# Banded lag products for a causal convolution and causal pooling, with token tiles arranged by phase

## The chip, the cores and the metric

The kernel runs on one core of a Trainium2 chip. The metric is the device time of one execution in microseconds. Each version is timed over several runs, and one execution is profiled.

## What is computed

One layer of a hybrid encoder on x of 2048 tokens by 1024 channels, in float32:

```
x  = LayerNorm(x)
h  = x @ w_in                       # 1024 -> 384 value | 384 gate | 384 pool | 256 query
a  = h_value * sigmoid(h_gate)
a  = causal_depthwise_conv(a, 31 taps) + bias
a  = silu(LayerNorm over the 384 channels of a)
p  = (trailing mean over 2/4/8/16 tokens, by group of 96 channels) - h_pool
p  = (p @ pool_w of its group) * scale
mo = 4-head attention from h_query into 256 memory tokens
y  = concat(a, p, mo) @ w_out
x  = LayerNorm(alpha * x + y)
u  = causal_depthwise_conv(x @ w_up, 3 taps) + bias   # 1024 -> 2 x 2816
y  = (silu(u_gate) * u_value) @ w_down
x  = LayerNorm(alpha * x + y)
```

The means of the first tokens divide by the number of tokens seen so far, not by the window.

## The kernel before

Every large product is made from three TensorE products. Each operand is split into a high part (a copy in the engine's 32-bit format, ScalarE) and a low part (the subtraction of the high part, VectorE), and high x high, high x low and low x high are summed in PSUM (`exact_parts`, L37). Each phase is a block of programs, one per engine, tied by semaphores. SP issues all DMAs. Order on an engine is program order.

**Input phase** (`input_phase`, L73). Four chunks of 512 tokens. At the start four tiles of x are normalised (statistics and affine on VectorE, L412 to L428; the reciprocal root on POOL; the scaling on ScalarE, L319), turned by TensorE (`turn`, L256) and split (L324, L441), and w_in is loaded in eight rows of 1408 columns, split at L371 and L528. TensorE then runs `project` (L281): 11 column tiles of 24 matmuls each. ScalarE evacuates them (`evacuate`, L326). The conv has three tiles of 128 channels. Two are convolved on VectorE, 31 steps of `scalar_tensor_tensor` per tile and chunk (`conv`, L458, the step at L473). The third is convolved on TensorE: ScalarE scales the identity by a tap's high and low part (`tap_matrix`, L346), and TensorE does 3 matmuls of 512 columns per tap (`last_tile_conv`, L269, matmul at L278), between the turns of the next chunk. Pooling runs on VectorE by doubling the window (`pool_level`, L484). Results go to the scratch `mix_d`, channels by tokens. The next chunk's LayerNorm stands ahead of the conv on VectorE.

**Mixing phase** (`mixing_phase`, L562). First the preparation: memory, key, value, pool and output weights are loaded (L730 to L753) and split (`prep_low` L1226, `wout_hi` L1044, `wout_lo` L1230). TensorE makes the keys (L918), folds the pool weights into the output weights (L935) and makes the values (L944). Then eight chunks of 256 tokens: scores, softmax, attention, the LayerNorm and swish of the conv result, the output projection, the residual and its LayerNorm. `chunk` (L949, L1083, L1269) gives the hand-written order of each engine: the projection of one chunk is mixed with the attention of the next. Chunk 0 runs without a projection beside it, and TensorE waits for all eight output weight tiles ahead of chunk 1 (`pe.wait_ge(wo_l, KT)`, in the lines after L949). x1 and sums of its quarters are stored.

**FFN phase** (`ffn_phase`, L1332). Both large products by a scheme of seven half-size products instead of eight (`product`, L1664). The up projection is done in two stages of 1024 tokens with 22 blocks each; a block is one 128-channel tile of gate and of value. Its width-3 conv is one ScalarE step (`first_tap`, L1764) and two VectorE steps for each of the two windows (`conv`, L1883), reading the tile shifted by 0, 1 and 2 columns. Two columns are saved to and restored from `up_carry` between the stages (`save_edge` L1752, `restore_edge` L1758). `keep_u2` (L1727) copies the second product, and TensorE waits for it ahead of the fourth.

The order of TensorE around a chunk of the input phase:

```
with pe.Fori(0, NCH - 1) as c:
    project(c)
    for n in range(2 * TT):
        turn(c + 1, n)
        for k in range(4 * n, min(4 * n + 4, CONV_K)):
            last_tile_conv(c, k)
project(NCH - 1)
for k in range(CONV_K):
    last_tile_conv(NCH - 1, k)
```

Of the kernel before, what the change touches and what calls it, by code (L numbers as in the profile page):

```python
# [5 lines left out]
F32 = mybir.dt.float32  # L6
# [56 lines left out]
POOL_ROWS = []  # L63
for _g, _w in enumerate(POOL_WINDOWS):
    _c = _g * POOL_GROUP
    while _c < (_g + 1) * POOL_GROUP:
        _p = _c % P
        _n = min((_g + 1) * POOL_GROUP - _c, P - _p, {0: 128, 32: 32, 64: 64, 96: 32}[_p])
        POOL_ROWS.append((_c // P, _p, _n, _w))
        _c += _n  # L70


def input_phase(nc, a, x0_d, mix_d, used):  # L73

# [4 lines left out]
    HALO = CONV_K - 1  # L81
    PH = max(POOL_WINDOWS)
    DT = CT - 1
    RING = 4
    GATE_AT, LOW_AT = 9, 12
    with ExitStack() as ctx:
        sb = lambda n, s, d=F32: ctx.enter_context(nc.sbuf_tensor(n, s, d))
        
# [5 lines left out]
        xt_hi = sb("x0t_hi", [P, KT, CH], F32R)  # L94
        xt_lo = sb("x0t_lo", [P, KT, CH], F32R)
        xs = sb("x_in", [P, 2, D])
        x0 = sb("x0", [P, TT, D])

        glu = sb("glu", [P, DT, HALO + CH])
        glt_hi = sb("glu_last_hi", [P, HALO + CH], F32R)  # L100
        glt_lo = sb("glu_last_lo", [P, HALO + CH], F32R)

        diag = sb("tap_diag", [P, RING, 2, P], F32R)
        cwt_hi = sb("tap_hi", [P, CONV_K], F32R)
        cwt_lo = sb("tap_lo", [P, CONV_K])

        vg = sb("val_gate", [P, 2, CT, PH + CH])

        cp = sb("conv_pool", [P, 2, CT * CH])
        pin = sb("pool_in", [P, CT, PH + CH])  # L110
        qb = sb("q_out", [P, QT, CH])
        g_b = sb("ln0_gb", [P, 2, D])
        cw = sb("conv_w", [P, CT, CONV_K])
        cb = sb("conv_b", [P, CT])
        ident = sb("ident0", [P, P])
        half = sb("rstd_consts0", [P, 2])
        st = sb("ln0_stats", [P, TT, 16])
        rc = sb("pool_recip", [P, CT, PH])
        rw = sb("pool_recip_full", [P, CT, PH])
        ptmp = sb("pool_head", [P, CT, PH])  # L120
# [3 lines left out]
        x_loaded = [sem(f"x_loaded{i}") for i in range(2)]  # L124
        x_first = [sem(f"x_first{i}") for i in range(TT)]
        raw_loaded = [sem(f"win_loaded{i}") for i in range(5)]
        consts = sem("consts0")
# [4 lines left out]
        ln_stats = sem("ln0_stats_done")  # L132
        ln_var = sem("ln0_var")
        half_ok = sem("half0_ok")
        pchain = sem("pool_chain0")
        x0_norm = sem("x0_norm_done")
        x0_ready = sem("x0_ready")
        x0_stored = [sem(f"x0_stored{i}") for i in range(TT)]
# [5 lines left out]
        conv_done = sem("conv_done")  # L144
        taps_hi = sem("taps_hi_done")
        taps_lo = sem("taps_lo_done")
        diag_ready = sem("diag_ready")
        last_gated = sem("glu_last_done")
        glt_hi_done = sem("glu_last_hi_done")
        glt_lo_done = sem("glu_last_lo_done")  # L150
        halo_hi = sem("halo_hi_done")
        tap_mm = sem("tap_mm_done")
        last_conv = sem("last_conv_done")
        pool_done = sem("pool_done")
        conv_stored = sem("conv_stored")
        pool_stored = sem("pool_stored")
        last_stored = sem("last_conv_stored")
        q_stored = sem("q_stored")
        chain = sem("dve_chain0")
        block = ctx.enter_context(nc.Block())  # L160


        order = [v for t in range(CT) for v in (t, CT + t)] + list(range(2 * CT, JT))

        def load_x(sp, c, u):
            if isinstance(c, int) and c == 0:

                sp.dma_start(x0[:, u, :], a["x"][u * P:(u + 1) * P, :]).then_inc(x_first[u], 16)
                return

            if not (isinstance(c, int) and c == 1 and u < 2):
                sp.wait_ge(x0_norm, c * TT + u - 1)
            sp.dma_start(xs[:, u % 2, :], a["x"][bass.ds(c * CH + u * P, P), :]).then_inc(x_loaded[u % 2], 16)

        def store_x0(sp, c, u):
            sp.wait_ge(x0_ready, c * TT + u + 1)
            sp.dma_start(x0_d[bass.ds(c * CH + u * P, P), :], x0[:, u, :]).then_inc(x0_stored[u], 16)

        def store_mix(sp, c):

            at = c * CH if isinstance(c, int) else sp.snap(c * CH)

            def rows(r, n):
                return mix_d[r:r + n * P, bass.ds(at, CH)].rearrange("(t p) s -> p t s", p=P)
            sp.wait_ge(conv_done, DT * (c + 1))
            sp.dma_start(rows(0, DT), cp[:, 0, 0:DT * CH].rearrange("p (t s) -> p t s", t=DT)).then_inc(conv_stored, 16)
            sp.wait_ge(evac, JT * (c + 1))
            sp.dma_start(rows(D_CONV + D_POOL, QT), qb[:, :, :]).then_inc(q_stored, 16)
            sp.wait_ge(pool_done, c + 1)
            sp.dma_start(rows(D_CONV, CT), cp[:, 1, :].rearrange("p (t s) -> p t s", t=CT)).then_inc(pool_stored, 16)  # L190
            sp.wait_ge(last_conv, c + 1)
            sp.dma_start(mix_d[DT * P:D_CONV, bass.ds(at, CH)], cp[:, 0, DT * CH:]).then_inc(last_stored, 16)

# [5 lines left out]
        def _(sp):  # L199
            def load_w(k):  # L200
                if k >= len(landing):

                    sp.wait_ge(win_lo, k - len(landing) + 1)
# [1898 lines left out]
```

## Time and profile before

| | |
|---|---|
| median of 3 runs | 2083.57 us (2080.91 to 2083.67) |
| profiled execution | 2081.61 us, its span 2079.8 us |
| TensorE busy | 1915.2 us, 92% of the span, 8584 matmuls |
| VectorE busy | 1637.7 us, 79% |
| ScalarE busy | 984.5 us, 47% |
| POOL busy | 218.6 us, 11% |
| mean granted TensorE clock | 0.969 |
| DMA | 282.96 MB, mean 136 GB/s |

The span is the time from the first to the last instruction. Busy times overlap, because the engines run side by side; a matmul's busy time includes its way through the pipeline, so the pitch from start to start says more. A granted clock of 1.00 is 2.4 GHz, 0.50 is 1.2 GHz. "Idle before" is the idle time of the engine ahead of the instructions of a row, with what ended it.

### The profile page before, as it was taken

To read this page: it belongs to the slowest core of one execution; us is meant where nothing else is said; L and a number is where in the kernel's file an instruction comes from. 1 tells how busy PE (TensorE), PEld (TensorE's weight loads), DVE (VectorE), ACT (ScalarE), POOL (GpSimd) and SP (SyncE) were. 2 spreads that over 40 slices of the span, in tenths; PEclk is the share of its full clock that TensorE was granted. 3 is DMA by queue.
4 is the path that set the end of the run, shared out by engine and by line. 5 is a ranking of instruction groups with operands and counts; after the bars stand their busy time and mean duration, and the time that the engine had idled before them with its cause. 6 is when DMAs were issued, how large, how long until landed. Compare 5 with 4: busy or idle time off the path is not lost.

```text
span 2079.8 us, 26573 instructions
## 1 busy us (share of the span) xinstructions
PE 1915.2 (92%) x8584; PEld 1580.4 (76%) x8584; DVE 1637.7 (79%) x2241; ACT 984.5 (47%) x1681; POOL 218.6 (11%) x263
## 2 busy tenths in 40 slices
PE   3999999669999849999999999999999798999997
PEld 2887878558878638888888778888888686887786
DVE  7979877568898557888888788777778767656899
ACT  4264351555555345555555655555555434324231
POOL 1010100001122201222122001000000000000111
PEclk9999999789999969999999999999999899999999
DMA  6130210523443363334434524222214557547543
GB/s 247 67 114 27 81 41 1 195 91 110 144 151 116 131 239 112 134 139 141 141 123 149 202 102 142 83 89 91 81 71 142 186 203 267 190 170 263 183 162 121
DMA packets 135506, 282.96 MB, mean 136 GB/s; under 512 B 10512, under 2 KB 66960, under 8 KB 135440
## 3 DMA queue, kind: packets, MB, share of 16 engines
q1 hardware_dynamic: 135440, 282.13, 38.3%
q8 instruction: 35, 0.57, 0.1%
q14 instruction: 31, 0.25, 0.0%
HBM read 182.48 MB, written 99.61 MB: 136 GB/s over the span
## 4 chain that ended last, share of the span: by engine, by line
PE 54%; DMA 4%; DVE 3%; issue 1%; ACT 1%; SPq 0%; DVEq 0%; ACTq 0%
PE prod_ps L1671 54%; DVE mov_lo L1852 1%; DMA y_scratch<-up_and_out 1%; DMA mov_raw<-wdown_sums_scratch 1%; DMA mov_raw<-x_operands 1%; ACT mov_hi L1718 1%; DVE sta_lo L1848 0%; DMA mov_raw<-in_ln_b 0%; DVE up_and_out L1888 0%; DMA mov_raw<-in_w_down 0%; DVE up_and_out L1885 0%; DMA up_and_out<-x_scratch 0%; ACT sta_hi L1711 0%; ACT prod_ps L1725 0%; DVE sta_raw L1864 0%
## 5 line engine op out<-in xcount | busy, mean ns | idle before, releaser
L1671 PE MATMUL prod_ps<-mov_hi,sta_hi 128*128 128x512 f32 x1848 | 727.5, 394 | 41.0 <-ACT prod_ps L1725 25.6
L1671 PE MATMUL prod_ps<-mov_lo,sta_hi 128*128 128x512 f32 x1848 | 725.5, 393 | 0.0
L1671 PE MATMUL prod_ps<-mov_hi,sta_lo 128*128 128x512 f32 x1848 | 725.2, 392 | 0.0
L1671 PEld LDWEIGHTS prod_ps<-mov_hi,sta_hi 128*128 128x128 f32 x1848 | 351.1, 190 | 119.6 <-ACT prod_ps L1725 27.7
L1671 PEld LDWEIGHTS prod_ps<-mov_hi,sta_lo 128*128 128x128 f32 x1848 | 350.8, 190 | 73.9
L1671 PEld LDWEIGHTS prod_ps<-mov_lo,sta_hi 128*128 128x128 f32 x1848 | 351.0, 190 | 73.3
L1848 DVE TENSOR_TENSOR sta_lo<-sta_raw,sta_hi 128x512 fp32r<-128x512 f32 (+1 forms) x340 | 223.5, 672 | 66.7 <-ACT sta_hi L1711 64.0
L1711 ACT ACTIVATE sta_hi<-sta_raw 128x512 fp32r<-128x512 f32 (+1 forms) x340 | 198.3, 611 | 161.7 <-PE prod_ps L1671 120.6
L473 DVE SCALAR_TENSOR_TENSOR conv_pool<-glu,conv_w,conv_pool 128x512 f32<-128x512 f32 x240 | 160.1, 746 | 0.0
L294 PE MATMUL wb<-x0t_hi,win_hi 128*128 128x512 f32 x352 | 137.6, 391 | 4.8 <-DVE win_lo L528 4.8
L294 PE MATMUL wb<-x0t_hi,win_lo 128*128 128x512 f32 x352 | 137.4, 390 | 0.0
L294 PE MATMUL wb<-x0t_lo,win_hi 128*128 128x512 f32 x352 | 137.4, 390 | 0.0
L1740 ACT ACTIVATE half_sums<-prod_ps 128x512 f32<-128x512 f32 x68 | 40.7, 599 | 181.0 <-PE prod_ps L1671 181.0
L1881 DVE TENSOR_TENSOR up_and_out<-prod_ps,half_sums 128x512 f32<-128x512 f32 x44 | 30.4, 691 | 121.4 <-PE prod_ps L1671 121.4
L1731 ACT ACTIVATE half_sums<-prod_ps 128x512 f32<-128x512 f32 x68 | 40.7, 598 | 176.5 <-PE prod_ps L1671 161.7
L1888 DVE SCALAR_TENSOR_TENSOR up_and_out<-up_and_out,ffn_conv_w 128x1024 f32<-128x1024 f32 x88 | 113.1, 1285 | 11.2 <-DVE up_and_out L1885 5.5
L1778 ACT ACTIVATE up_and_out<-up_and_out,ffn_conv_b,ffn_conv_w 128x1024 f32<-128x1024 f32 x88 | 108.8, 1236 | 7.9 <-ACT up_and_out L1750 5.2
L1885 DVE SCALAR_TENSOR_TENSOR up_and_out<-up_and_out,ffn_conv_w 128x1024 f32<-128x1024 f32 x88 | 112.5, 1279 | 0.0
L908 PE MATMUL y_ps<-wout_hi,mix_hi 128*128 128x512 f32 x256 | 102.6, 401 | 0.5 <-DVE mix_lo L1196 0.5
L908 PE MATMUL y_ps<-wout_hi,mix_lo 128*128 128x512 f32 x256 | 99.9, 390 | 0.0
L908 PE MATMUL y_ps<-wout_lo,mix_hi 128*128 128x512 f32 x256 | 99.7, 389 | 0.0
L1848 DVE TENSOR_TENSOR sta_lo<-sta_sums,sta_hi 128x512 fp32r<-128x512 f32 (+1 forms) x136 | 90.8, 668 | 0.0
(241 smaller groups left out, 2788.4 us busy)
## 6 DMA issues: line engine op xcount, KB each, us to landing
sta_raw<-in_w_up SPq DMA_DIRECT2D x88, 512.0 KB, 4.2
hidden_scratch<-up_and_out SPq DMA_DIRECT2D x44, 512.0 KB, 2.6
y_scratch<-up_and_out SPq DMA_DIRECT2D x16, 1024.0 KB, 7.3
sta_raw<-hidden_scratch SPq DMA_DIRECT2D x32, 512.0 KB, 4.4
up_and_out<-y_scratch SPq DMA_DIRECT2D x16, 1024.0 KB, 4.9
x_operands<-x_operands_out SPq DMA_DIRECT2D x56, 256.0 KB, 3.8
mov_raw<-x_operands SPq DMA_DIRECT2D x14, 1024.0 KB, 7.0
mov_raw<-in_w_down SPq DMA_DIRECT2D x44, 256.0 KB, 4.5
```

What stands on the lines that cost most here:

```text
L294: last = pe.matmul(wb[:, n % 6, :], w, x, start=(k == 0 and i == 0), stop=(k == KT - 1 and i == 2))
L473: ins = dve.scalar_tensor_tensor(out=conv_of(t), in0=src, scalar=cw[:, t, k:k + 1], in1=conv_of(t), op0=ALU.mult, op1=ALU.add)
L908: last = pe.matmul(ps_y[:, b, :], w, x, start=(k == 0 and i == 0), stop=(k == KT - 1 and i == 2))
L1671: last = pe.matmul(psum, w, x, start=(start and k == 0 and i == 0), stop=(stop and k == m - 1 and i == 2), skip_group_check=True)
L1711: act.activation(sa_hi[:, j, 0:PAIRS[b.st], :], held(b, j), ACT.Copy).then_inc(sta_hi[j], 1)
L1731: act.activation(u[:, 0, :], ps[:, 2 + b.r, :], ACT.Copy).then_inc(u2, 1)
L1740: act.activation(u[:, 1, :], ps[:, 2 + b.r, :], ACT.Copy).then_inc(u4, 1)
L1778: act.activation(cv[:, w, :], ub[:, w, 0:HT], ACT.Identity, scale=fw[:, w, bass.ds(b.i, 1), 0], bias=fb[:, w, bass.ds(b.i, 1)]).then_inc(t ...
L1848: dve.tensor_tensor(sa_lo[:, j, 0:m, :], held(b, j), sa_hi[:, j, 0:m, :].bitcast(F32), ALU.subtract).then_inc(sta_lo[j], 1)
L1881: dve.tensor_tensor(tokens(b, VALUE, 0), bank(4 + b.r), u[:, 0, :].rearrange("p (q t) -> p q t", t=P), ALU.add).then_inc(c21, 1)
L1885: dve.scalar_tensor_tensor(out=cv[:, w, :], in0=ub[:, w, 1:1 + HT], scalar=fw[:, w, bass.ds(b.i, 1), 1], in1=cv[:, w, :], op0=ALU.mult, op ...
L1888: dve.scalar_tensor_tensor(out=cv[:, w, :], in0=ub[:, w, 2:2 + HT], scalar=fw[:, w, bass.ds(b.i, 1), 2], in1=cv[:, w, :], op0=ALU.mult, op ...
```

## The change

**Tokens by phase.** Each half of the sequence (1024 tokens) is read as 128 rows of 8 phases: token tile r of a half holds the tokens 8q + r, for q from 0 to 127. All later tiles, chunks and scratches keep that order, and the output is written back through the same stride.

**Input phase** (now `project_phase`). It only normalises, turns and projects, with two buffers of turned activations, all four chunks written out without a loop, and the turns of the next chunk between the column tiles of this one. The LayerNorm is two passes on VectorE with the root on POOL. w_in, its columns reordered by the host, comes in ten pieces: four of 512 columns first, then three of 512, then three of 384. The slots of tiles 4 and 5 of x serve as landing room for pieces. VectorE multiplies value by gate, and the gated values and pool inputs go to a new scratch `cp_d` by phase.

**Mixing phase.** 48 groups of 16 channels are put into the preparation, 24 for conv and 24 for pooling. A group's 128 partitions are 16 channels x 8 phases, and its 256 columns are q of both halves. A causal window is then a sum over lags s of band_s (128 x 128) times the group shifted by s columns: five lags with three products each for conv (15 matmuls of 256 columns), two or three lags with two products for pooling (4 or 6). The host lays out the conv bands (128 x 640 per group, loaded), ScalarE makes their high parts and **POOL their low parts**. The pooling bands are built by POOL with selects. The first two columns of a pool group are corrected by three small VectorE operations. The output weight tiles 3 to 7 are now split after chunk 0.

**FFN phase.** The conv reads the tile shifted by 0, 128 and 256 columns, with an edge of 256 columns filled by two ScalarE copies per window and block.

```
-            def last_tile_conv(c, k):
...
-            def conv(c):
...
-            def pool_level(c, lvl):
...
+            def project(c, n):
+                done = c * JT + n
+                if n == 0:
+                    pe.wait_ge(lo_done, 2 * TT * (c + 1))
+                if c == 0 and n in (0, 4, 8):
+                    pe.wait_ge(win_lo, {0: 4, 4: 7, 8: 10}[n])
...
+            for c in range(NCH):
+                for n in range(JT):
+                    project(c, n)
+                    if c + 1 < NCH and 1 <= n <= 2 * TT:
+                        turn(c + 1, n - 1)
...
+            def load_x(n):
+                if n in (4, 5):
+                    sp.wait_ge(win_lo, len(pieces))
...
+            for c in range(NCH):
+                for n in range(JT):
+                    evacuate(c, n)
+                    if c == 0 and n == 1:
+                        for i in range(7, 10):
+                            weights_hi(i)
...
+            layer_norm(0)
+            layer_norm(1)
+            layer_norm_end(0)
+            layer_norm(2)
+            layer_norm_end(1)
+            weights_lo(0)
+            lows(0, 0, 1)
+            layer_norm(3)
+            layer_norm_end(2)
+            weights_lo(1)
+            lows(0, 2, 3)
+            layer_norm_end(3)
+            weights_lo(2)
+            lows(0, 4, 5)
+            weights_lo(3)
+            lows(0, 6, 7)
...
+            def load_group(n):
+                if n >= 4:
+                    sp.wait_ge(gx_lo, n - 3)
+                if n >= 4 + CONV_GROUPS:
+                    sp.wait_ge(g_fix, n - 3 - CONV_GROUPS)
...
+            def load_taps(n):
...
+                if n >= 3:
+                    sp.wait_ge(gt_lo, n - 2)
...
+            for n in range(NG):
+                if n + 4 < NG:
+                    load_group(n + 4)
+                load_taps(n + 3)
...
+                if n:
+                    store_group(n - 1)
...
+            def taps_lo(n):
+                pool.wait_ge(gt_hi, n + 1)
...
+                pool.tensor_tensor(l, gt_raw[:, n % 3, :], h.bitcast(F32), ALU.subtract).then_inc(gt_lo, 1)
...
+            def group(n):
+                pe.wait_ge(gx_lo, n + 1)
...
+                    pe.wait_ge(gt_lo, n + 1)
+                    for s in range(LAGS):
+                        cols = slice(LEAD - s, LEAD - s + QS)
+                        for i, (w, x) in enumerate(exact_parts(gt_h[:, n % 3, s, :], gt_l[:, n % 3, s, :], gx_h[:, slot, cols], gx_l[:, slot, cols])):
+                            last = pe.matmul(bank, w, x, start=(s == 0 and i == 0), stop=(s == LAGS - 1 and i == 2))
...
+            for n in range(NG):
+                group_out(n)
+                if n + 3 < NG:
+                    group_hi(n + 3)
+                    taps_hi(n + 3)
...
             query_lo(0, 0)
             chunk(0, 0, None, None)
+            for n in range(CT, KT):
+                wout_lo(n)
             chunk(1, 1, 0, None)
...
+            def fill_edge(b, w):
...
+                act.activation(first[:, :, 1:P], last[:, :, 0:P - 1], ACT.Copy).then_inc(edge[w], 1)
+                if b.st == 0:
+                    act.activation(kept, last[:, :, P - 1:P], ACT.Copy).then_inc(edge[w], 1)
+                else:
+                    act.activation(first[:, :, 0:1], kept, ACT.Copy).then_inc(edge[w], 1)
```

## Rows read from the trace of the kernel before

**Rows 1.** Busy time by stretch: PE, PEld, DVE, ACT, POOL busy (instructions), clock, DMA share, GB/s

```profile
104.00:384.80 280.80, 276.62 (x1253) 226.59 (x1251) 224.67 (x358) 128.99 (x321) 13.28 (x24) 1.00 0.15 55
...
388.40:413.70 25.30, 8.54 (x48) 8.37 (x48) 15.09 (x16) 9.46 (x10) 0.67 (x5) 0.61 0.93 317
...
432.10:461.80 29.70, 14.51 (x63) 11.56 (x64) 17.52 (x32) 16.08 (x33) 0.00 (x0) 0.71 0.12 37
```

**Rows 2.** Groups by line, 0 to 385 us: count, busy us, mean ns, idle before

```profile
L473 DVE SCALAR_TENSOR_TENSOR conv_pool<-glu,conv_w,conv_pool 128x512 f32<-128x512 f32 x240 | 160.1, 746 | 0.0
L294 PE MATMUL wb<-x0t_hi,win_hi 128*128 128x512 f32 x352 | 137.6, 391 | 4.8 <-DVE win_lo L528 4.8
...
L278 PE MATMUL wb<-glu_last_hi,tap_diag 128*128 128x512 f32 x248 | 84.0, 403 | 3.8 <-ACT tap_diag L354 3.8
...
L266 PE MATMUL tp<-ident,x 128*128 128x128 f32 x128 | 23.0, 312 | 28.1 <-DVE x0t_lo L441 15.9 <-DVE x L426 12.2
L441 DVE TENSOR_TENSOR x0t_lo<-tp,x0t_hi 128x512 fp32r<-128x512 f32 x32 | 21.7, 685 | 17.1 <-ACT x0t_hi L324 16.7
```

**Rows 3.** Instructions in order of time, 0 to 70 us: start, duration, engine

```profile
0.73 0.87 SPq L168 DMA_DIRECT2D x<-in_x  x2
...
4.40 0.69 DVE L419 BATCH_NORM_STATS2 ln_stats<-x 128x6 f32<-128x512 f32 x1 [3.14 <-DMA x<-in_x]
...
5.72 0.21 DVE L421 BATCH_NORM_AGGREGATE ln_stats<-ln_stats 128x2 f32<-128x12 f32 x1
...
9.59 1.22 DVE L425 TENSOR_TENSOR x<-x,ln_gb 128x1024 f32<-128x1024 f32 x1 [2.27 <-DMA ln_gb<-in_ln_b]
...
40.30 0.76 PE L294 MATMUL wb<-x0t_hi,win_hi 128*128 128x512 f32 x1 [4.77 <-DVE win_lo L528]
...
40.86 0.63 PE L294 MATMUL wb<-x0t_lo,win_hi 128*128 128x512 f32 x1
...
41.29 0.63 PE L294 MATMUL wb<-x0t_hi,win_lo 128*128 128x512 f32 x1
...
61.45 0.39 PE L294 MATMUL wb<-x0t_hi,win_hi 128*128 128x512 f32 x1
...
69.39 0.39 PE L294 MATMUL wb<-x0t_hi,win_lo 128*128 128x512 f32 x1
```

**Rows 4.** Groups by line from 385 us on, and one instruction beside POOL's

```profile
L1888 DVE SCALAR_TENSOR_TENSOR up_and_out<-up_and_out,ffn_conv_w 128x1024 f32<-128x1024 f32 x12 | 15.4, 1285 | 1.6 <-DVE up_and_out L1885 0.8
...
L804 POOL TENSOR_TENSOR x_operands_out<-x_operands_out 128x512 f32<-128x512 f32 x8 | 10.5, 1315 | 75.2 <-ACT x_operands_out L1081 75.2
...
L1233 DVE TENSOR_TENSOR wout_lo<-x_out,wout_hi 128x1024 fp32r<-128x1024 f32 x4 | 4.9, 1219 | 1.2 <-ACT wout_hi L1047 1.2
...
L1047 ACT ACTIVATE wout_hi<-x_out 128x1024 fp32r<-128x1024 f32 x4 | 4.2, 1050 | 3.4 <-DMA x_out<-in_w_out 3.4
...
L1018 ACT ACTIVATE conv_rstd<-moment_ps,eps 128x256 f32<-128x256 f32 x8 | 3.8, 474 | 0.1
...
L1756 ACT ACTIVATE up_carry<-up_and_out 128x4 f32 x12 | 2.5, 208 | 1.6
...
570.57 1.56 DVE L1176 TENSOR_TENSOR conv_sum<-conv_sum,conv_sq 128x256 f32<-128x256 f32 x1
```

**Rows 5.** DMA issues: SP's instructions in time, and KB each with median us to landing

```profile
968.69 1.96 SPq L1535 DMA_DIRECT2D wdown_sums_scratch<-mov_raw  x4
...
wdown_sums_scratch<-mov_raw SPq DMA_DIRECT2D x88, 128.0 KB, 1.7
...
sta_raw<-hidden_scratch SPq DMA_DIRECT2D x16, 384.0 KB, 3.8
```

**Rows 6.** TensorE in order of time, 425 to 430 us, matmuls of 256 columns

```profile
425.12 0.28 PE L944 MATMUL probT_ps<-probT_lo,mix_hi 128*128 128x256 f32 x1
...
429.44 0.28 PE L944 MATMUL probT_ps<-probT_lo,mix_hi 128*128 128x256 f32 x1
```

**Rows 7.** Waits, 900 to 2079 us: us in total, times, longest

```profile
ACT half_sums L1731 <- PE prod_ps L1671: 146.7, 56, 4.2
```

More of the change, by code:

```diff
@@ L156, in input_phase @@
-        pool_stored = sem("pool_stored")
-        last_stored = sem("last_conv_stored")
+        gated = sem("gated_done")
+        glu_stored = [sem(f"glu_stored{i}") for i in range(CT)]
+        pin_stored = sem("pool_in_stored")
         q_stored = sem("q_stored")
-        chain = sem("dve_chain0")
         block = ctx.enter_context(nc.Block())
[L163 to L192, printed above, removed]
@@ L565, in mixing_phase @@
+def mixing_phase(nc, a, x0_d, cp_d, mix_d, x1_d, xop_d, used):
     CH = 256
@@ L774, in _ @@
             turn_over(1, 1)
-            with sp.Fori(1, NCH // 2 - 1) as h:
+            for h in range(1, NCH // 2 - 1):
                 turn_over(h * 2, 0)
@@ new lines, in _ @@
+            pool.wait_ge(counts_ok, 1)
+            for i, w in enumerate(POOL_WINDOWS):
+                for t in range(w - 1):
+                    last = pool.memset(counts[:, 2 * i + t // PHASES, t % PHASES:t % PHASES + 1], w / (t + 1))
+            last.then_inc(counts_ok, 1)
+            for n in range(3):
+                taps_lo(n)
+            rows = "p (c r) -> p c r"
+            link(pool.memset(same, 1.0))
+            same_cr = same.rearrange(rows, r=PHASES)
+            link(pool.affine_select(out=same_cr, in_=same_cr, compare_op=ALU.is_ge, fill=0.0, base=0,
+                                    pattern=[[-PHASES, GROUP], [0, PHASES]], channel_multiplier=1))
@@ new lines, in keys @@
+            def keys():
+                pe.wait_ge(prep_lo, 2)
+                for t in range(QT):
+                    for k in range(KT):
+                        cols = slice(t * P, (t + 1) * P)
+                        for i, (w, x) in enumerate(exact_parts(wk_hi[:, k, cols], wk_lo[:, k, cols], memT_hi[:, k, :], memT_lo[:, k, :])):
+                            last = pe.matmul(ps_s[:, t, 0:MEM], w, x, start=(k == 0 and i == 0), stop=(k == KT - 1 and i == 2))
+                    last.then_inc(prep_mm, 1)
@@ L1299, in _ @@
             chunk(0, 0, None, None)
+            for n in range(CT, KT):
+                wout_lo(n)
             chunk(1, 1, 0, None)
```

944 lines of the change are left out of this document (506 added, 438 removed).

## The prediction

> **What bounds the kernel now.** I read the busy times by stage first, because the change touches the stages unequally. Stage 1 (input projection, convolution, pooling) runs to 384.8 us, the preparation and the first chunk of stage 2 to 461.8 us, and the rest is left nearly alone. Stage 1 has TensorE busy for 276.6 of 280.8 us between 104 and 384.8, and VectorE for 224.7 [rows 1]. The groups of instructions by line say with what: 240 tap steps of 746 ns on VectorE for two conv tiles, 372 tap matmuls on TensorE for the third (31 taps x 3 x 4 chunks; the row of 248 holds two of the three), and 1056 projection matmuls (352 in each of three rows) [rows 2]. So TensorE is the bound of stage 1, and what leaves it there shortens the stage. The preparation is different: from 388.4 to 413.7 the DMA engines are busy 0.93 of the time and TensorE 8.5 of 25.3 us at a granted clock of 0.61 [rows 1]. That is where the change puts the new work.
>
> **Stage 1 after the change.** Everything of conv and pooling goes: 372 matmuls, the tap matrices of ScalarE, the tap steps and pooling of VectorE.
> The start is a chain on VectorE, whose program order I add up. The scale vector lands at 9.59 us [rows 3]. From there: 8 affine passes over 1024 columns at 1.285 us (nearest: the FFN conv step, the same operation and width) = 10.3; statistics of three more tiles at 2 x 0.68 + 0.21 = 4.7; four low parts of weights at 1.22 = 4.9; eight of the turned activations at 0.685 = 5.5 [rows 2 to 4]. Sum 25.4, so the first projection matmul starts at 35.0 where it now starts at 40.3.
> Projection matmuls start every 0.2267 us (61.45 to 69.39 is 35 pitches) [rows 3]: 1056 x 0.2267 = 239.4. The 24 turns inside take 0.72 each (23.0 us for 32 [rows 2]), 17.3. The cold start costs 3 as now: the first matmuls of 512 columns start every 0.43 us (40.86 to 41.29), at half the clock [rows 3]; I bound it by 1 and 4.
> Then **a new stall**. After two column tiles of chunk 0 TensorE must turn tile 4 of x. That tile's slots hold weights until all ten pieces are split. The last three pieces' high parts stand on ScalarE behind the evacuation of the second column tile. So: tiles 0 and 1 end at 35.0 + 3 + 10.9 = 48.9; evacuation 0.6; high parts of 3072 columns at 1.05 per 1024 = 3.2; last low part 0.5; load of x 3.7 (first x: issued at 0.73, used at 4.40); statistics 1.6; two affine passes 2.6; semaphores 0.5. That ends at 61.6, 12.7 late; with two more for the clock that drops meanwhile, 15 [rows 3, 4]. Nothing else can cover it, because TensorE works in order.
> The end: last matmul, evacuation 0.6, store of 512 KB and the change of phase; now 3.6 from the last matmul to the next phase (384.8 to 388.4) [rows 1], with the longer store behind it I take 5.
> 35.0 + 239.4 + 17.3 + 3 + 15 + 5 = 314.7 against 388.4: **-73.7** (between -66 and -82, the latter if most of the stall is not there).
>
> **The 48 groups in the preparation.** Each has a load of 128 KB, two stores of 64 KB, and for conv a load of 320 KB of bands; each is a pipeline SP, ScalarE, VectorE or POOL, TensorE, ScalarE, SP. Prices:
> - SP issues a DMA every 0.48 us (four in 1.96 [rows 5], a little of it a wait): four per conv group, 1.9; three per pool group, 1.4.
> - The DMA engines ran at 317 GB/s while 0.93 busy [rows 1], 341 at full share: 0.59 MB per conv group, 1.7; besides, 4.2 MB of other loads are issued among them, 12.3 in all.
> - TensorE: 15 matmuls of 256 columns at 0.12 (425.12 to 429.44, 36 pitches [rows 6]) = 1.8 at 2.4 GHz; at 1.2 GHz half of the 0.43 of 512 columns [rows 3], 0.215 each, 3.2. Pool groups: 4 to 6, at most 0.7, or 1.3 at the low clock.
> - ScalarE: 0.47 out, 0.40 high part (0.47 is the row for 256 columns), 0.75 for 640 columns of bands (between 0.47 for 256 and 1.05 for 1024) = 1.6 [rows 4].
> - POOL, the low part of the bands: 512 columns take 1.315 us, so 640 take 1.5; for nine groups two or three selects come on top, bounded by 0.2 and 1.0. VectorE would take about 0.8 for the same. While POOL subtracts, VectorE's sum of 256 columns took 1.56 us [rows 4], over twice the 0.685 that 512 columns take elsewhere [rows 2]; VectorE has one such subtraction per conv group, which the other engines cover. If the cover were gone it would cost 1.1 x 24 = 27.
>
> No engine alone exceeds 2 us a conv group; what ties them is the slot count. A band slot frees when POOL has subtracted, three groups ahead: issue 0.5 behind the group load and two stores (1.4), landing 3.3 (nearest: 128 KB 1.7 us, 384 KB 3.8 us [rows 5]), high part 0.75, evacuation in the same queue 0.47, semaphores 0.3: 6.7 us for three groups, 2.2 each. With 12.3 us of foreign loads in the way, I take 2.5: 24 x 2.5 = **60** (bounds 24 x 1.9 = 46, and 77 with TensorE at 1.2 GHz).
> Pool groups: the load for group n+4 waits until group n's first two tokens are corrected; ScalarE then has its high part ahead of the evacuation of n+2. So two groups per loop: landing 2.3, high part 0.4, evacuation 0.4, three linked tiny VectorE operations 0.7, semaphores 0.3 = 4.1, 2.05 each; 24 give 49. Keys (48 matmuls, 5.8), key, weight and fold splits are put into the same queues; I add 5. **54** (bounds 31, at 1.3 each and without the splits, and 66).
> Filling the pipeline: 8 (5 to 11). Groups in all: 8 + 60 + 54 = 122, then the fold can begin. Today the fold begins 25.3 after the phase [rows 1]: **+96.7**, since the work of those 25.3 us is now inside.
> From the fold to the end of chunk 0 nothing changes. Then five tiles of the output weights are split only now, and TensorE may not start chunk 1 before. The last of them is loaded after the first is split: 1.05 + 1.22 + load 3.8 + 1.05 + 1.22 + semaphores 0.5 = **+9** (bounds 6 and 12), at a place where TensorE goes straight on now [rows 4, 5].
>
> **FFN.** Each block gets four small ScalarE copies for the edges (0.47 for the wide pair, 0.21 for the narrow pair [rows 4]) in place of one of 0.21, some 1.0 us more per block. ScalarE waits 146.7 us in 56 blocks on TensorE before it keeps the second product [rows 7], 2.6 each: covered, 0. If the cover were gone it would be 44 x 1.0 = 44. Row-strided loads and stores of x and the output keep 4 KB rows: 0.
>
> **Sum.** -73.7 + 96.7 + 9 = +32 on the profiled execution's 2081.6: 2113.6. That execution is 2.0 under the median of the runs, so I forecast **2115**.
>
> **Two rules of the Trainium skill against this.** Stores of 128 KB and loads of 384 KB land after 1.7 and 3.8 us [rows 5], and I let them overlap. "DMA: Bandwidth & Descriptors", section Bandwidth, asks for transfers of about 1 MiB and says small ones are dominated by descriptors: 64 KB takes 0.95 us. By it, as an estimate, the DMA work of a conv group would be above 3.5 us, 24 groups 84, the sum some 24 us higher.
> The clock rows show 0.61 and 0.71 where TensorE worked in pieces [rows 1]. "TensorE: Matmul & The Clock Gate", section on why it matters for kernels, warns that gaps between bursts bring the clock back to its low level; by that a conv group costs 3.2 on TensorE and the sum is 17 higher.
>
> **The rivals.**
> *The groups run at their engines' floors* (faster). Latency hides, the in-flight loads are enough: conv 1.9, pool 1.3, filling 6: 83, so +57.5; wout +7; stage 1 at -77: -12, 2071. It decides below about 90 us of groups. For it: no single engine needs more. Against: the loops above contain landing times, which the slots do not cover. Chance 0.22.
> *Transfers or the low clock bound the conv groups* (slower still). Conv groups at 3.2, TensorE's price at 1.2 GHz [rows 3], 77 instead of 60; pool groups 2.5, when their loads land in 3.3 instead of 2.3, 12 more: +32 + 17 + 12 = +61, 2144 with the 2.0 to the median 2145. For it: the DMA share of 0.93 in this place; TensorE in pieces. Against: at the low clock TensorE would be busy all the time, and such stretches are granted 1.00 [rows 1]. Chance 0.14.
> *It cancels*: groups 96 and no stall in stage 1, within 4 us of 2083.6. Chance 0.06.
> *FFN loses its cover*: ScalarE late in half the blocks, 20 more, 2135. Chance 0.04. The window's waits speak against.
> The forecast itself (2095 to 2130): 0.54.
>
> **Numbers.** A measurement of this kernel tells about 0.2%, 4 us, from no change. Faster 0.22, same 0.06, slower 0.72. The range leaves out the lower half of the first rival and the top of the second: 2074 to 2142. The likeliest case alone would span 2095 to 2130.
>
> **What the new profile would show.** First projection matmul near 35 us; TensorE idle some 13 us after 48 projection matmuls, released by VectorE's x; the last projection matmul near 310; 48 groups over some 120 us with ScalarE or TensorE waiting on DMA loads; pool groups at 2 us with TensorE's clock at its low level; TensorE idle 9 us after chunk 0; FFN blocks of the same length. The forecast is wrong if the groups take under 95 us, or if projection has no stall and the groups no DMA waits.

## The result, and the profile after

The kernel after takes 2114.97 us (median of 4 runs, 2113.01 to 2117.23), the kernel before on the same chip 2082.78. The ratio is 1.0156, 95% interval 1.0138 to 1.0174: slower by 32 us, where 2115 was forecast in a range of 2074 to 2142. Its profiled execution took 2117.23 with a span of 2115.5.

Cut at four dates, the two spans (2079.8 and 2115.5) differ by

| from, to | before | after | difference | forecast |
|---|---|---|---|---|
| start to end of stage 1 | 388.4 | 308.1 | -80.3 | -73.7 |
| to the first matmul of the fold | 25.3 | 127.7 | +102.4 | +96.7 |
| fold to the first product of the FFN | 336.7 | 349.0 | +12.3 | +9 |
| FFN | 1329.4 | 1330.8 | +1.4 | 0 |
| sum | | | +35.8 | +32 |

Busy time by stretch, the view of [rows 1], shows where the new stages sit (columns: stretch, length, PE, PEld, DVE, ACT, POOL busy with instructions, clock, DMA share, GB/s):

```profile
33.50:61.20 27.70, 14.02 (x49) 11.03 (x49) 13.11 (x13) 8.25 (x9) 1.59 (x2) 0.79 0.59 215
61.20:304.10 242.90, 242.88 (x1104) 200.49 (x1104) 67.27 (x90) 36.41 (x65) 17.54 (x22) 0.99 0.23 76
308.00:314.90 6.90, 0.00 (x0) 0.01 (x1) 2.55 (x6) 1.89 (x4) 3.34 (x33) 0.59 0.69 205
314.90:382.00 67.10, 51.54 (x361) 48.72 (x362) 37.38 (x38) 38.99 (x77) 51.34 (x48) 0.92 0.84 256
382.00:435.70 53.70, 31.08 (x158) 25.56 (x156) 25.33 (x100) 21.53 (x55) 0.00 (x0) 0.68 0.46 131
435.70:454.00 18.30, 15.55 (x90) 13.71 (x91) 5.80 (x15) 5.88 (x16) 0.00 (x0) 1.00 0.76 272
454.00:491.70 37.70, 15.20 (x57) 12.01 (x57) 22.65 (x36) 20.30 (x37) 0.00 (x0) 0.62 0.21 73
```

Read it line by line. From 61.2 to 304.1 TensorE never stops, but all of it is projection. Ahead of that it is busy for only half of 27.7 us. The conv groups (314.9 to 382) have four resources between 48 and 56 us of 67: TensorE (51.5), POOL (51.3), the DMA engines (0.84 x 67.1 = 56) and SP (101 issues in 48.5 us, which are not counted as busy). The pool groups (382 to 435.7) have none above 31 us of 53.7 (TensorE 31.1, SP 30.4 for 69 issues): a stage without a busy resource is a chain of waits. So the waits come next: TensorE's, from 30 to 500 us (line waited, releaser, us in total, times, longest):

```profile
PE probT_ps L887 <- POOL wout_lo L754: 14.1, 6, 10.8
PE tp L235 <- DVE x L334: 13.7, 1, 13.7
PE probT_ps L896 <- DVE wout_lo L1278: 12.1, 10, 3.2
PE scores_ps L807 <- DVE wout_lo L1273: 8.8, 1, 8.8
```

L235 is the turn of tile 4, L887 a conv group, L896 a pool group, L807 the scores of chunk 1. SP's own waits from 382 to 436 us name the loop of the pool groups: the loads (L609) wait on the last operation of the correction of the first two tokens (L1289):

```profile
SPq L609 <- DVE x_operands_out L1289: 20.7, 13, 3.8
SPq L627 <- DVE x_operands_out L1289: 2.1, 6, 0.4
```

A landing is the time from SP's issue of a transfer to the arrival of its data. The landings in the conv groups (314 to 378 us; KB each, median us from issue to landing), to be held beside the 1.7 of 128 KB and 3.8 of 384 KB in [rows 5]:

```profile
x_operands_out<-in_conv_bands SPq DMA_DIRECT2D x21, 320.0 KB, 4.0
x_operands_out<-conv_pool_in_scratch SPq DMA_DIRECT2D x22, 128.0 KB, 3.8
mix_scratch<-x_operands_out SPq DMA_DIRECT2D x42, 64.0 KB, 3.5
```

### The profile page after: what moved, and what is told of

Same layout as the page of the kernel before. It is cut to its first block, busy times and chain, and to the rows that moved or that the text cites. A ratio compares the mean times of both kernels' runs of the same rounds, so it can differ in the third digit from the quotient of the medians.

```text
span 2115.5 us, 26458 instructions
## 1 busy us (share of the span) xinstructions
PE 1908.6 (90%) x8680; PEld 1582.2 (75%) x8680; DVE 1475.7 (70%) x1954; ACT 963.3 (46%) x1657; POOL 265.8 (13%) x323
## 4 chain that ended last, share of the span: by engine, by line
PE 54%; DMA 4%; DVE 3%; issue 1%; ACT 1%; SPq 0%; DVEq 0%; ACTq 0%
PE prod_ps L1761 54%; DVE mov_lo L1943 1%; DMA y_scratch<-up_and_out 1%; DMA mov_raw<-wdown_sums_scratch 1%; DMA mov_raw<-x_operands 1%; ACT mov_hi L1808 1%; DVE up_and_out L1977 0%; DMA mov_raw<-in_w_down 0%; DVE up_and_out L1974 0%; DMA mov_raw<-in_ln_b 0%; DVE sta_lo L1939 0%; DMA up_and_out<-x_scratch 0%; ACT sta_hi L1801 0%; ACT prod_ps L1815 0%; DVE up_and_out L1994 0%
## 5 line engine op out<-in xcount | busy, mean ns | idle before, releaser
L1761 PE MATMUL prod_ps<-mov_hi,sta_hi 128*128 128x512 f32 x1848 | 727.8, 394 | 42.7 <-ACT prod_ps L1815 27.7
L1761 PEld LDWEIGHTS prod_ps<-mov_hi,sta_lo 128*128 128x128 f32 x1848 | 350.7, 190 | 73.7
L1970 DVE TENSOR_TENSOR up_and_out<-prod_ps,half_sums 128x512 f32<-128x512 f32 x44 | 30.4, 691 | 122.4 <-PE prod_ps L1761 122.4
```

The lines of the kernel that those rows point to most:

```text
L1761: last = pe.matmul(psum, w, x, start=(start and k == 0 and i == 0), stop=(stop and k == m - 1 and i == 2), skip_group_check=True)
L1970: dve.tensor_tensor(tokens(b, VALUE, 0), bank(4 + b.r), u[:, 0, :].rearrange("p (q t) -> p q t", t=P), ALU.add).then_inc(c21, 1)
```

## The experiments

Twelve kernels, all made from the kernel after. Three questions: are the waits above what costs the time; what sets the pace of the conv groups (the loop over band slots, bytes, POOL, SP's issues); and do the mends together beat the kernel before. The length of the two group stages is read from the first starts of their matmuls: the conv stage runs from the first matmul of a conv group to the first of a pool group, the pool stage from there to the first of the fold. Each ratio is to runs of the kernel before that were made beside it (medians 2081.6 to 2083.0 us). The same stretch differs from one run to the next. In the kernel after and in the four runs that left the conv groups alone (e1, e5, e6, e9) the conv stage took 67.1, 68.2, 66.3, 64.2 and 67.1 us: a single run tells some 3 us there, not less. The stretch from the fold to the FFN, 349.0 in the kernel after, is 345.5 to 348.5 in the seven runs that left it alone (e1 to e5, e7, e9), and the FFN is between 1327.3 and 1331.7 in all. The pool stage of the eight kernels that left it alone (or, e7, nearly so) lies between 52.6 and 53.7.

| run | conv stage | pool stage | median us | ratio to before, interval |
|---|---|---|---|---|
| after | 67.1 | 53.7 | 2114.97 | 1.0138 to 1.0174 |
| e1 late turns | 68.2 | 53.6 | 2101.02 | 1.0072 to 1.0106 |
| e2 low parts on VectorE | 67.5 | 52.6 | 2110.07 | 1.0115 to 1.0149 |
| e3 8 columns of bands | 63.5 | 53.3 | 2110.65, one run | |
| e4 four band slots | 62.4 | 53.5 | 2105.97 | 1.0102 to 1.0136 |
| e5 first two tokens kept | 66.3 | 41.4 | 2102.17 | 1.0084 to 1.0118 |
| e6 output weights early | 64.2 | 52.6 | 2111.58 | 1.0128 to 1.0159 |
| e7 one store | 65.6 | 53.6 | 2112.47 | 1.0129 to 1.0160 |
| e8 all mends | 58.0 | 36.8 | 2076.15 | 0.9949 to 0.9977 |
| e9 edge copies twice | 67.1 | 53.3 | 2113.07 | 1.0138 to 1.0169 |
| e10 mends, POOL low parts | 62.6 | 36.9 | 2082.06 | 0.9993 to 1.0011 |
| e11 loads moved | 58.6 | 40.4 | 2079.32 | 0.9978 to 0.9996 |
| e12 loads after bands | 51.4 | 46.7 | 2082.96 | 0.9991 to 1.0009 |

**e1, the stall of stage 1.** On TensorE and ScalarE:

```diff
-                    if c + 1 < NCH and 1 <= n <= 2 * TT:
-                        turn(c + 1, n - 1)
+                    first = 3 if c == 0 else 1
+                    if c + 1 < NCH and first <= n < first + 2 * TT:
+                        turn(c + 1, n - first)
```

> In chunk 0 alone the eight turns of chunk 1 stand behind column tiles 3 to 10 instead of 1 to 8, on TensorE and ScalarE alike. If the stall of 13.7 us behind the first turn is a missed date of tile 4 of x (its slot holds weights until all ten pieces are split), two more column tiles of 5.45 us are done meanwhile: stall 13.7 - 10.9 = about 3, the last projection ends 10 to 12 us earlier (304.1 to about 293), total 2115 to about 2104. Rival: the chain behind x is pushed back by the later turns, because VectorE's order ties gates, norms and low parts together; then the stall shows again at the gates or at the next tiles and the end of the projection moves by less than 4 us.

The stall fell from 13.7 to 3.1 us:

```profile
PE tp L235 <- DVE x L336: 3.1, 1, 3.1
PE wb L250 <- DVE x0t_lo L342: 2.9, 2, 1.5
```

The last projection matmul starts at 292.7 instead of 303.7. The median is 14 us lower, of which 11 are in this stage. The date of tile 4 did not move with the turns: its turn comes at 60.4, where it came at 61.2. It is fixed by the weights' slots, since SP's load of that tile waits for the last low part of the weights (kernel after, 20 to 64 us):

```profile
SPq L144 <- DVE win_lo L345: 13.4, 1, 13.4
```

So the turn had been placed two column tiles too early, and the rival (the chain moves along) is out.

**e2, who makes the low parts of the bands.** The same subtraction, in VectorE's order behind `group_lo`:

```diff
-                pool.tensor_tensor(l, gt_raw[:, n % 3, :], h.bitcast(F32), ALU.subtract).then_inc(gt_lo, 1)
+                dve.tensor_tensor(l, gt_raw[:, n % 3, :], h.bitcast(F32), ALU.subtract).then_inc(gt_lo, 1)
```

> The low parts of the bands are made by VectorE, right behind each group's low part, instead of by POOL. My theory (a loop over three band slots: issue, landing 4.0, high part, low part 1.64 on POOL, semaphores, in all about 8.5 us for three groups): the low part falls from 1.64 to about 0.8, so 0.28 less per group, conv stage 67 to about 60. The group's own low part falls from 0.72 to about 0.4 us, since POOL no longer subtracts beside it. Rival 1, the DMA queues bind (0.59 MB per group and 4 MB of others at some 300 GB/s): conv stage within 2 us of 67. Rival 2, POOL is the bound in its nine groups with selects: conv stage falls by 10 or more. Rival 3, VectorE becomes the bound: slower.

Half of the expectation came: POOL went from 51 to 9 us busy, the bands' low part from 1.64 to 0.82, and the group's low part takes 0.36 to 0.55 us. The stage did not move (67.5 against 67.1) where 60 was expected: that is the mark set for rival 1, the DMA queues, which e3 then speaks against. The landing of the bands grew from 4.0 to 4.5. The median is 4.9 lower, though the intervals of the ratios overlap, so no gain and no loss is shown. Two instructions of VectorE in order of time, of the kernel after and then of e2:

```profile
315.65 1.58 DVE L1278 TENSOR_TENSOR wout_lo<-x_operands_out,wout_hi 128x256 fp32r<-128x256 f32 x1 [0.59 <-ACT wout_hi L1049]
319.31 0.43 DVE L1278 TENSOR_TENSOR wout_lo<-x_operands_out,wout_hi 128x256 fp32r<-128x256 f32 x1 [2.08 <-ACT wout_hi L1049]
```

```profile
317.90 0.43 DVE L1270 TENSOR_TENSOR wout_lo<-x_operands_out,wout_hi 128x256 fp32r<-128x256 f32 x1 [1.64 <-ACT wout_hi L1041]
318.53 0.82 DVE L1277 TENSOR_TENSOR wout_lo<-x_operands_out,wout_hi 128x640 fp32r<-128x640 f32 x1 [0.20 <-ACT wout_hi L1049]
```

In the kernel after the first of them stands beside two subtractions on POOL (315.39 to 318.6), the second beside POOL's selects with one input, which cost it nothing. The rows say that the instruction which begins second waits. The seven single ones of VectorE that began while POOL subtracted took 1.15 to 1.77 us, and each ended 0.27 to 0.33 us after POOL's. One began 0.02 us before POOL's: it took 0.42, and POOL's took 1.81 instead of some 1.55:

```profile
323.35 0.42 DVE L1278 TENSOR_TENSOR wout_lo<-x_operands_out,wout_hi 128x256 fp32r<-128x256 f32 x1 [1.34 <-ACT wout_hi L1049]
323.37 1.81 POOL L754 TENSOR_TENSOR wout_lo<-x_operands_out,wout_hi 128x640 fp32r<-128x640 f32 x1
```

The Trainium skill, "GPSIMD Engine Reference", section Specifications, says that POOL shares its SBUF interfaces with VectorE, with contention where VectorE's instruction has two SBUF inputs; the rows agree.

**e3, bytes taken away.** From the fourth group on, 8 of 640 columns of bands are loaded. The kernel leaves out most of the convolution's weights and computes with the bands of the first groups:

```diff
-                sp.dma_start(gt_raw[:, n % 3, :], a["conv_bands"][n * P:(n + 1) * P, :]).then_inc(gt_in[n % 3], 16)
+                w = LAGS * P if n < 3 else 8
+                sp.dma_start(gt_raw[:, n % 3, 0:w], a["conv_bands"][n * P:(n + 1) * P, 0:w]).then_inc(gt_in[n % 3], 16)
```

> From the fourth conv group on only 8 of the 640 columns of bands are loaded, so these groups compute with bands of the first three (part of the convolution's weights is left out). Number of DMAs, instructions and waits are the same; 21 x 316 KB = 6.8 MB of 18 MB are not moved. If moving bytes binds (DMA share 0.84, landing 4.0 us), conv stage 67 to 50 or less and SP or POOL are the next bound (SP issues about 111 DMAs at 0.47 = 52 us). If SP's issues and its order bind already, or POOL, the conv stage stays above 60.

6.8 MB less moved, DMA share 0.56 and landings of 2.0 us bought 3.6 us. So in the kernel after bytes alone don't set the pace. Nor does the slot loop by itself: its landing is 2 us shorter, which over three slots would be 0.7 a group, some 15 us in all. SP now waits most for POOL's low parts:

```profile
313.00:372.00 59.00, 42.63 (x307) 40.66 (x308) 34.83 (x34) 35.36 (x71) 49.30 (x47) 0.92 0.56 159
```

```profile
SPq L619 <- POOL wout_lo L755: 8.4, 9, 1.7
SPq L611 <- DVE wout_lo L1279: 3.9, 4, 2.2
SPq L628 <- ACT x_operands_out L1065: 2.8, 4, 1.3
```

**e4, a fourth slot for the bands** (raw, high and low, in memory that is free then; loads go one group further ahead):

```diff
-                if n >= 3:
-                    sp.wait_ge(gt_lo, n - 2)
+                if n >= 4:
+                    sp.wait_ge(gt_lo, n - 3)
...
-                load_taps(n + 3)
+                load_taps(n + 4)
```

> A fourth slot for the bands, raw, high and low, in memory that is free then; loads go one group further ahead. Slot loop theory: about 8.5 us now over four groups is 2.1 each, the next bound (DMA 2.2 to 2.35, POOL 2.1 with its selects, SP four issues 1.9) takes over: conv stage 67 to 54 to 58. Rival, DMA throughput binds already: within 2 us of 67, and the bands' landing grows from 4.0 to above 5. Pool groups unchanged at 54.

62.4: 4.7 less (1.8 less than the shortest unchanged run), which is half of the least that the slot loop promised (9) and more than the rival allowed. ScalarE's wait for bands went from 19.1 us to 2.1 (after, then e4):

```profile
ACT wout_hi L1057 <- DMA x_operands_out<-in_conv_bands: 19.1, 12, 3.3
```

```profile
ACT wout_hi L1052 <- DMA x_operands_out<-conv_pool_in_scratch: 3.9, 4, 1.7
ACT wout_hi L1060 <- DMA x_operands_out<-in_conv_bands: 1.5, 4, 0.4
ACT wout_hi L1060 <- DMA x_in<-in_conv_bands: 0.6, 2, 0.5
```

The loop over slots was real, and the next bound stood 5 us behind it. What that bound is, e10 and e8 tell.

**e5, the loop of the pool groups.** VectorE keeps the first two tokens, the correction reads the copy, and the load no longer waits for it:

```diff
-                if n >= 4 + CONV_GROUPS:
-                    sp.wait_ge(g_fix, n - 3 - CONV_GROUPS)
...
+                if n >= CONV_GROUPS:
+                    dve.tensor_copy(first_two[:, n % 4, :], gx_raw[:, n % 4, 0:2]).then_inc(kept, 1)
```

> VectorE copies a pool group's first two tokens before its low part, and the correction reads the copy; so the load for group n+4 waits only for the low part of group n and not for its correction. Theory (the slot loop with the correction in it takes 4.1 us for two groups): it goes, and pool groups run at the next bound, SP's three issues or ScalarE with the inserted splits, 1.4 to 1.6 each: pool stage 53.8 to 36 to 40, total -15. Rival: the splits and keys in the same queues bind, or the in-order SP that waits for the correction before it stores: pool stage falls by less than 5 us. The 24 copies of 0.06 to 0.15 us cost nothing.

53.7 to 41.4, the median 12.8 us lower: as expected in size, a little short of 36 to 40. What is left on SP is the store behind the correction:

```profile
SPq L627 <- DVE x_operands_out L1292: 7.9, 10, 3.2
SPq L611 <- DVE wout_lo L1280: 4.0, 10, 1.0
```

**e6, output weights early.** `wout_hi` and `wout_lo` of tile 0 (the fourth to be split) stand ahead of the fold's evacuations, of tiles 1, 2 and 6 ahead of chunk 0, only tile 7 behind it.

> Output weight tiles 0, 1, 2 and 6 are split ahead of chunk 0 (tile 0 ahead of the fold's evacuations, the others behind the value projection), only tile 7 stays behind it. Theory: TensorE's wait of 8.8 us ahead of chunk 1 goes but for some 2 us; ScalarE and VectorE do the splits in a stretch where TensorE is busy 15 of 38 us, but on the chain that ends chunk 0, so some 2 to 4 us come back there: total -3 to -6. Rival: the three tiles ahead of chunk 0 add all of their 3 x 1.2 us and wait for landing besides: no gain, within 2 us.

The wait ahead of chunk 1 is 2.9 instead of 8.8, and a wait at the first scores grew from 2.7 to 5.8:

```profile
PE scores_ps L807 <- issue: 5.8, 1, 5.8
PE scores_ps L807 <- DVE wout_lo L1275: 2.9, 1, 2.9
```

From the fold to the FFN it takes 345.2, 3.8 less than in the kernel after but level with the lowest of the seven runs that left this stretch alone (345.5), and the median is 3.4 lower with overlapping intervals. So the shorter wait is shown, a gain in the total is not.

**e7, one store for two** (128 KB in one DMA, runs of 512 bytes as before):

```diff
-                for h in range(2):
-                    dst = mix_d[h * D + n * GROUP:h * D + (n + 1) * GROUP, :].rearrange("c (r q) -> (c r) q", r=PHASES)
-                    sp.dma_start(dst, g_res[:, n % 4, h * P:(h + 1) * P]).then_inc(g_stored[n % 4], 16)
+                dst = mix_d[0:2 * D, :].rearrange("(h c) (r q) -> (c r) h q", h=2, r=PHASES)[n * P:(n + 1) * P]
+                sp.dma_start(dst, g_res[:, n % 4, :].rearrange("p (h q) -> p h q", h=2)).then_inc(g_stored[n % 4], 16)
```

> The two stores of 64 KB of a group are one DMA of 128 KB with the same runs of 512 bytes. SP issues three DMAs for a conv group instead of four. Theory (slot loop with SP's issues in it, not bytes alone): 0.5 less of about 8.5 us for three groups, conv stage 67 to 63 to 65; pool groups, whose loop ran over the correction, less than 2 us shorter in all. Rival, bytes bind alone: conv stage within 1 us of 67. Rival, SP binds alone: 24 x 0.47 = 11 us less, conv stage 56.

65.6, above the 63 to 65 expected and inside the scatter of unchanged runs. It excludes that SP's issues alone are the bound (56), and doesn't tell the theory from the bytes.

**e8, all of these together** (e1, e2, e4, e5, e6, e7).

> Together: late turns of chunk 1, low parts of the bands on VectorE, four band slots, first two tokens kept, output weights early, one store per group. By the single runs: 2115 - 11 (turns) - 5 (slots) - 13 (first two) - 4 (weights) - 5 (one store, in the conv stage with four slots and in the pool stage) = 2077, 5 us under the kernel before. If bytes bind the conv stage it ends at 18.2 MB / 310 GB/s = 58 us; if SP bound it with four slots it falls to 50 to 55. If the gains hide each other the total stays above 2083.

2076.15 us (5 runs, 2073.28 to 2077.22), ratio 0.9963: faster than the kernel before as well. The mends add up (by the medians of e1, e4, e5 and e6 alone 14 + 9 + 13 + 3 = 39 us against 38.8), though some of each is scatter. The conv stage, 58.0, is 9 shorter, where e4 brought 4.7 and e2 and e7 nothing that could be told. The conv groups of e8, and their landings (302 to 358 us):

```profile
303.70:361.60 57.90, 48.78 (x360) 47.93 (x361) 40.05 (x62) 39.60 (x77) 10.43 (x18) 0.90 0.90 293
```

```profile
x_operands_out<-in_conv_bands SPq DMA_DIRECT2D x15, 320.0 KB, 4.5
x_operands_out<-conv_pool_in_scratch SPq DMA_DIRECT2D x23, 128.0 KB, 4.4
mix_scratch<-x_operands_out SPq DMA_DIRECT2D x21, 128.0 KB, 5.2
```

**e9, the cover of the FFN.** Each of the 44 up blocks copies its edges once more, into a spare place:

```diff
+                act.activation(spare[:, :, 1:P], last[:, :, 0:P - 1], ACT.Copy).then_inc(again, 1)
+                act.activation(spare[:, :, 0:1], last[:, :, P - 1:P], ACT.Copy).then_inc(again, 1)
```

> Each of the 44 up blocks of the FFN issues four more small ScalarE copies (the edges again, into a spare place): about 2 x (0.47 + 0.21) = 1.4 us of ScalarE more per block. Theory (the FFN is TensorE's, and ScalarE waits 2.2 us per block on it): FFN from 1329.4 to at most 1332, total within 2 us of 2115. Rival (the cover is used up by the copies that the change brought): 44 x 1.4 = 60 us more. Between them: 44 x 0.3 = 13 if only a few copies stand ahead of something that TensorE waits for.

2113.07: nothing. ScalarE's busy time from the first blocks of the FFN to 1900 us grew from 607.8 to 639.3, its waits for the second product (the instruction of [rows 7], here in a shorter window) fell from 108.5 to 89.6, TensorE's busy time stayed (1079.4 and 1080.1). The cover holds twice the copies.

**e10, all mends but POOL makes the low parts.**

> The kernel with all mends, but POOL makes the low parts of the bands as in the kernel after. Once slots and SP's issues no longer set the pace, POOL's 24 x 1.64 plus 12 us of selects (51 us) and VectorE's low parts of the groups slowed beside it come near the stage of 57.9 us. Theory (coupled queues): conv stage 58 to 61, total 2 us over the 2076 of all mends. Rival, bytes set the pace there (DMA share 0.90): within 1 us of 57.9. Rival, POOL is a bound of its own: over 62.

2082.06 (10 runs) against 2076.15, and the intervals of the ratios (0.9993 to 1.0011, 0.9949 to 0.9977) lie apart. The conv stage is 62.6 instead of 58.0, and SP's wait ahead of the loads of bands is on POOL:

```profile
303.40:365.80 62.40, 49.39 (x359) 47.57 (x360) 35.95 (x39) 39.33 (x77) 51.11 (x48) 0.92 0.88 270
```

```profile
SPq L622 <- POOL wout_lo L758: 13.3, 12, 2.7
SPq L615 <- DVE wout_lo L1286: 6.2, 4, 3.7
```

More than the 2 us expected, and over the 62 that was set as the mark of POOL as a bound of its own. What e2 could not show, because the slot loop lay above it, is here: the placement of the low parts on POOL, without an effect on the stage in the kernel after, costs some 4.6 us once the rest is mended. It also settles what stopped e4. e4 (62.4) and e10 (62.6) both have four slots and the low parts on POOL, and e10 has one store per group fewer: the store made no difference that could be told there, and the step to 58.0 is that of the low parts, the only difference between e10 and e8.

**e11 and e12, the loads that are not of conv.** e11 moves three of them (two output weight tiles and the value weights), and a third output weight tile, by 3 to 6 groups in SP's order.

> All mends, and 2 MB of the loads that are not of conv (two output weight tiles and the value weights) are issued 3 to 9 groups later, near the end of the conv stage or among the pool groups, and split there. If bytes bind the conv stage with all mends (share 0.90 at 292 GB/s), it falls from 57.9 by up to 2 MB / 310 GB/s = 6.5 to 52 to 54, and the pool stage (36.9) grows by 1 to 3: total 2073. If queues bind it, conv stage stays within 2 us of 57.9, and the splits only make the pool stage longer: total 2077 or more.

The conv stage stayed (58.6) and the pool stage grew by 3.6, the marks of the rival. But the theory was not tested: SP runs up to four groups ahead, and two output weight tiles and the value weights still moved within the conv stage (287 GB/s, share 0.91). e12 puts all five behind the last bands, their splits with them, and the keys behind the ninth pool group:

```diff
-                if n == 3:
+                if n == 20:
                     sp.dma_start(r_memT, a["memT"].rearrange("(k p) m -> p k m", p=P)).then_inc(land[0], 16)
-                if n == 6:
+                if n == 22:
                     sp.dma_start(r_wk, a["w_mk"].rearrange("(k p) m -> p k m", p=P)).then_inc(land[1], 16)
```

> All mends, and the five large loads that are not of conv (two of the memory keys, the value weights, two output weight tiles, 4 MB) are issued only behind the last load of bands; their splits stand among the pool groups and the keys behind the ninth pool group. In the run before, SP ran so far ahead that three of them still moved within the conv stage. If bytes set the pace of the conv stage with all mends (17 MB at 293 GB/s, share 0.90), it falls from 57.9 towards TensorE's 49: 50 to 53, at a DMA share of 0.85 or less in its first three quarters. The pool stage then carries 10 MB and grows from 36.9 to 40 to 43. Total 2072 to 2076. If the queues bind it instead (SP in order, ScalarE, landing), it stays within 2 us of 57.9, and the total is 2079 or more.

The conv stage fell to 51.4 as expected, with TensorE busy for 46.6 of it: with all mends the loads had set its pace. That it was their bytes is likely, 14.25 MB in place of 17.0, but not isolated: two of the loads (2 MB) still moved in its last part, and the splits of the memory and the key weights (1.9 us each on ScalarE, 2.3 to 2.7 on VectorE) left the stage with them. The pool stage grew by 9.9 to 46.7, more than the 3 to 6 expected, and the total is 2082.96: 7 us worse than e8, where 2072 to 2076 was expected. The two stretches of e12, and SP there (303 to 400 us): its stores wait on the corrections, and behind them stand the loads.

```profile
303.00:350.00 47.00, 42.21 (x327) 41.51 (x327) 31.99 (x54) 32.80 (x70) 10.51 (x17) 0.93 0.88 271
350.00:400.00 50.00, 32.76 (x192) 29.31 (x190) 33.81 (x130) 28.24 (x62) 0.00 (x0) 0.78 0.75 233
```

```profile
SPq L630 <- DVE x_operands_out L1297: 21.6, 15, 5.6
```

What makes the pool stage lose more than the conv stage won (9.9 against 6.6) was not taken apart further: splits, keys and loads all moved together. e8 stays the fastest.

## Why the prediction was right, step by step

- **Stage 1, -73.7, measured -80.3.** The first projection matmul came at 33.5 (35.0). The stall was 13.7 (12.7, one event, released by VectorE's x), and e1 shows its cause. The end (last matmul to the next phase) took 4.0 (5). The rest is turns, cold start and clock, priced at 17.3 + 3 + 2.3 (what the 15 holds beyond the stall): 304.1 - 33.5 - 239.4 - 13.7 leaves 17.5. So -1.5, +1.0, -1.0, -5.1: the last is the mis-sized term. The 96 transposes of the 24 turns within the projection are busy for 14.9 us, 0.62 a turn; the 0.72 came from a row that also holds the eight turns of the slow start. Cold start and clock took 2.6 where they were given 5.3.
- **Filling, 8, measured 6.9.** One wait of 10.8 us on POOL's first low part covers the change of phase as well.
- **Conv groups, 60, measured 67.1** (2.8 each instead of 2.5). The step that failed is the sum of the slot loop: issue, landing 3.3, high part, evacuation, semaphores leaves out POOL's own subtraction, which frees the slot, and takes landings from an idle queue. With the measured 4.0 and 1.64 it is 0.5 + 1.4 + 4.0 + 0.74 + 0.47 + 1.64 + 0.3 = 9.05 for three groups, 3.0 each; measured 2.8. The 2.5 also held only half of the 0.5 a group that the 12.3 us of foreign loads come to. That the loop was the first bound, e4 shows, by ScalarE's waits for bands (19.1 to 2.1 us) more than by the 4.7 us. That its terms don't simply subtract, e2 and e3 show: the next bound, POOL's low parts (e10), stands 5 us behind it, and a landing is no constant. It is 2.0 us for the bands of e3 (4 KB) and 4.0, 4.5 and 4.5 in after, e2 and e8: in e2 what the slot gained came back in part as a longer landing.
- **Pool groups, 54, measured 53.7.** Right in size and cause: e5 takes the correction out of the loop and 12.3 us go. The loop's landing, put at 2.3, was 2.1.
- **+9 ahead of chunk 1, measured 8.8 of wait, but +12.3 in all.** Some of the 12.3 is scatter: the seven runs with the same wait and the same stretch have +8.8 to +11.8. Some is the clock. In the 38 us behind the wait the granted clock is 0.93, where the same stretch of the kernel before has 1.00, some 2.7 us; in the seven runs it is 0.93 to 0.96. It does not go by the length of the wait: in e6, where the wait is 2.9, the clock behind it is 0.92. The rows of the kernel after and of e6:

```profile
491.70:530.00 38.30, 38.30 (x182) 32.28 (x183) 26.73 (x45) 19.07 (x38) 2.03 (x6) 0.93 0.20 69
```

```profile
484.24:522.50 38.26, 38.26 (x180) 32.29 (x181) 26.33 (x45) 18.68 (x37) 2.03 (x6) 0.92 0.20 70
```

- **FFN, 0, measured +1.4**, within what two executions differ by (1327.3 to 1331.7 in the thirteen kernels); e9 shows the cover.
- **POOL beside VectorE, 0 (27 if the cover is gone).** The slowing is real, from 0.43 to between 1.15 and 1.77 us for 256 columns, and in e2 the stage is no shorter without it. e10 against e8 is the price once the slot loop is mended, 4.6 us, with POOL's slower subtraction in it.
- **The rivals.** Groups at their engines' floors (83): the measured groups are 127.7; without the filling 120.8, and even e8 needs 94.8 there, against 77 of the rival. Transfers as the bound (conv 77): not in this kernel (e3), likely in e8 (e12). The low clock: the conv stage had 0.92, not 0.50. The pool stage had 0.68, and e5 made it 12.3 us shorter at nearly the same clock, 0.71. The cancelling rival needed groups of 96 and no stall. The estimate by the Trainium skill's "DMA: Bandwidth & Descriptors", section Bandwidth, was 84 us for the conv groups; the trace has 67.1, with 256 GB/s at a share of 0.84 (305 at full share). Small transfers were dearer than the idle queue's rows say, and cheaper than by that figure.

That the median came within 0.1 us of the forecast is luck. The total was closer than its parts: stage 1 was 6.6 too dear, the groups 5.7 and the stretch from the fold to the FFN 3.3 too cheap, the FFN 1.4. What is left, 3.8, is there in the profiled execution (2117.23) and mostly gone in the median, which lies 2.3 below it, where 2.0 above had been added.

## What to carry to other kernels

When work is taken out of a stage with a busy engine and set into one that moves data, cost the new place by its loops: list what must happen before a slot is free, every operation up to the one that frees it, and divide by the slots. The pool stage, in which no resource was busy for more than 60%, was such a loop, and SP's own waits named the operation that closed it: the correction of two tokens held a 128 KB load and cost 12 us. Mend the first bound before judging the second: the engine that makes the bands' low parts made no difference to the conv stage under the slot loop, and 4.6 us in it and 6 in the total once that was mended.

## What the runs showed of the hardware that was not expected

- A landing depends on what else is in flight: 64 KB stores took 3.5 us in the conv groups at a DMA share of 0.84 and 1.8 in the pool groups of e5 at 0.59. The Trainium skill, "DMA: Bandwidth & Descriptors", section Latency and other measured facts, says that the latency of memory grows under load; the rows agree in direction.
- The clock behind a short wait does not follow its length: 0.93 over 38 us behind a wait of 8.8 us, 0.92 behind one of 2.9 (e6), 1.00 in the kernel before, where TensorE goes straight on.
- VectorE's subtraction of 256 columns takes 0.43 us beside POOL's selects. When it begins while POOL subtracts it ends about 0.3 us after POOL, whatever is left of POOL's 1.55, so it takes up to 1.77; when it begins first it takes 0.42, and POOL's is the longer, 1.81.
